# Rows for four more tokens in place of eight in an expert layer, with four buffers for spilled activations

## The chip, the cores and the metric

The kernel runs on one core of a Trainium2 chip. The metric is the device time of one launch in microseconds (us). Before the change the median of three runs is 3247.73 us (3247.13 to 3249.23).

## What is computed

The reference is a decoder trunk of two layers on 512 tokens of width 1024, in float32. Each layer has a block of three attention branches with gates, and then an expert block; the change touches the expert block alone:

```python
def peer_ffn(xn, w_q, k1, k2, u, v):
    # 8 heads, top 16 of 256 candidates each: 128 of 16384 experts for each token
    ...
        ids = jnp.take_along_axis(cand_id, top_pos, axis=-1)
        g = jax.nn.softmax(top_s, axis=-1)
        act = jnp.einsum('thk,td->thk', u[ids], xc, preferred_element_type=jnp.float32)
        w = (g * jax.nn.gelu(act, approximate=False)).astype(v.dtype)
        return jnp.einsum('thk,thkd->td', w, v[ids], preferred_element_type=jnp.float32).astype(xn.dtype)
```

## The kernel before

Each of the 512 tokens uses 128 experts, so for most tokens the kernel computes all 16384 experts densely and multiplies with a gate table that is zero where a token doesn't use an expert. TensorE does this for the first TM = 344 tokens: 344 is the number of columns of each product. The other 168 go "by rows": one indirect DMA by GpSimd gathers 128 rows of `u` or `v` (128x1024 float32, 0.52 MB), and VectorE makes a dot product or an addition of them. The last 128 tokens take one such operation for each of their 128 experts. E = 32 further tokens take 32 (four partitions for each token), and F = 8 more take 8 (16 partitions for each): KF = P // F = 16 copies of the 8 tokens' activations fill the 128 partitions of `x_f`. `row_of` lists these row operations: 2 x (32 + 128 + 8) = 336 in a layer, half with `u`, half with `v`.

A weight chunk holds 256 experts (1 MB). There are 64 up chunks (`u`, then Gelu) and 64 down chunks (`v`), one in each step q of 0 to 127. Every product is three matmuls of float32r parts (hi*hi, hi*lo, lo*hi; `product`, lines 1506 to 1508), 16 products in a chunk, so a chunk is 48 matmuls. Each chunk is loaded by SyncE's queue (`load_raw`) into one of two `raw` buffers when VectorE is done with the chunk two before; ScalarE rounds it to `hi` (`split_hi`, L626), VectorE subtracts (`split_lo`, L983, 2.3 us), then TensorE can use it.

The steps of a layer, by q: 0 to 13 up chunks while the experts are being found; 14 to 42 up chunks with the making of the gate table beside them (three groups of four tokens in a step; a group is two one-hot tables and four 128x128 matmuls, L1815; 86 groups in 29 steps, so the first step has two); 43 to 51 up chunks; then rounds of six down and six up chunks, down at 52 to 57, 64 to 69 and 76 to 81; from 82 on down chunks alone. The Gelu outputs of the first SPILLED = 46 up chunks are spilled to `act_d` in DRAM (`store_act`, 352 KB each); those of the last KEPT = 18 stay in `act_k`, `act_s`, `act_in`. A down chunk needs its activations multiplied by the gates (`weigh_step`), split (`weights_hi` on ScalarE, `weigh_lo` on VectorE) and then TensorE takes them.

SyncE's queue issues in a fixed order. In the down steps from q = 80 on that is: `load_raw` of the chunk, `load_act` of the same chunk's activations into `act_in[s]` (two buffers; it waits until the chunk two before is weighed), and one of four parts of the gates for four chunks (`load_gates`). Before that, `GATES_AT` says at which q parts of gates are loaded; (0, 0) and (0, 2) at 50 and 51 stand for two parts each, so the first block of gates is issued at q = 50 and 51. Four parts have 1.4 MB, in pieces of 1 KB.

VectorE and GpSimd run through the row operations in one fixed order. `rows_by(q)` says how many VectorE has done by the end of step q: 96 of them in steps 14 to 42, and the other 240 in steps 43 to 125 by weights of 16 for an up step and 13 for a down step. GpSimd gathers up to NR = 7 rows ahead: gather n waits until VectorE is done with row n - 7. Before gather n == F_IN = 40 GpSimd issues, in its own instruction order, two small DMAs and the KF loads that make `x_f` (line 606). VectorE waits for a row inside its own stream (`row_op`), in front of the next one-hot tables and the next `split_lo`.

## Time and profile before

| what | before |
|---|---|
| median of three runs | 3247.73 us |
| the profiled execution, as timed | 3249.34 us |
| its span, first to last instruction | 3247.5 us |
| mean granted TensorE clock | 0.998 of 2.4 GHz |
| moved by DMA | 893 MB, mean 275 GB/s |

The profiled execution is 1.6 us longer than the median, and 1.8 us of it lie outside the span. The profile lists for each engine the time in which it was busy, for each idle time the event that ended it, and for each stretch how much was moved by DMA. A matmul's listed duration overlaps the next one's, so the cost of a matmul is read from the distance between two starts in the list by time, not from its duration.

### The profile page before, as it was taken

Reading aid. Unit: us, or ns where it says so; the run is one execution under the profiler, and the core shown is the slowest. Engines: PE = TensorE matmul, PEld = TensorE weight load, DVE = VectorE, ACT = ScalarE, POOL = GpSimd, SP = SyncE. Lnnn points to the kernel's source line nnn. Section 1 sums busy time; section 2 is a strip of 40 time slices with the busy share of each in tenths; the row PEclk is TensorE's granted clock in tenths of the full one; section 3 lists DMA queues with packets and bytes.
Section 4 is the critical chain, followed back from the end, with each engine's and each line's share of the span. In section 5 each row is a group of like instructions: output and inputs, shape, how many; then the busy total and the mean of one; then the engine's idle time right before and its main releaser. Section 6 shows DMA issues by size and latency. Waiting matters only on the chain.

```text
span 3247.5 us, 54682 instructions
## 1 busy us (share of the span) xinstructions
PE 3202.2 (99%) x19694; PEld 3000.9 (92%) x19694; DVE 2597.5 (80%) x4972; ACT 1508.2 (46%) x2298; POOL 1191.4 (37%) x789
## 2 busy tenths in 40 slices
PE   8999999999999999999999999999999999999998
PEld 7878888999999999999988788889999999999998
DVE  6654449999998889999866544499999888999997
ACT  5553233477773333333345532334777633333333
POOL 1000014335435656555300000143454456665552
PEclk9999999999999999999999999999999999999999
DMA  4214422589999999999821143225999999999996
GB/s 148 78 53 143 142 90 91 194 326 386 400 398 399 357 389 390 413 409 416 310 91 66 53 156 130 97 100 189 346 391 393 405 393 370 390 398 417 415 411 258
DMA packets 232172, 893.29 MB, mean 275 GB/s; under 512 B 23856, under 2 KB 69088, under 8 KB 184128
## 3 DMA queue, kind: packets, MB, share of 16 engines
q1 hardware_dynamic: 112912, 455.25, 37.2%
q0 software_dynamic: 99024, 355.98, 27.8%
q10 hardware_dynamic: 20064, 79.91, 6.2%
q8 instruction: 90, 1.47, 0.2%
q14 instruction: 82, 0.67, 0.1%
HBM read 809.57 MB, written 81.48 MB: 274 GB/s over the span
## 4 chain that ended last, share of the span: by engine, by line
PE 63%; issue 14%; DMA 12%; DVE 8%; POOL 2%; ACT 1%; SPq 0%; DVEq 0%; POOLq 0%; ACTq 0%
PE bank L1506 18%; PE bank L1508 18%; PE bank L1507 18%; DMA act_in<-act_d 9%; PE bank L1815 4%; DVE h L1383 4%; DVE w_lo L1411 2%; POOL lo L568 1%; PE bank L1624 1%; PE bank L1661 1%; DMA rows<-in_u_rows,ids 1%; PE bank L1642 1%; DMA raw<-in_stream 1%; DVE lo L983 1%; ACT hi L626 1%
## 5 line engine op out<-in xcount | busy, mean ns | idle before, releaser
L626 ACT ACTIVATE hi<-raw 128x2048 fp32r<-128x2048 f32 (+2 forms) x338 | 620.6, 1836 | 692.9 <-PE bank L1508 396.1
L1506 PE MATMUL bank<-xT_hi,hi 128*128 128x344 f32 (+1 forms) x2688 | 918.7, 342 | 2.1 <-DVE xT_lo L1033 1.7
L1508 PE MATMUL bank<-xT_hi,lo 128*128 128x344 f32 (+1 forms) x2688 | 905.1, 337 | 0.0
L1507 PE MATMUL bank<-xT_lo,hi 128*128 128x344 f32 (+1 forms) x2688 | 900.3, 335 | 0.0
L983 DVE TENSOR_TENSOR lo<-raw,hi 128x2048 fp32r<-128x2048 f32 (+2 forms) x320 | 698.4, 2183 | 183.1 <-ACT hi L626 180.9
L1506 PE MATMUL bank<-w_hi,hi 128*128 128x344 f32 x2048 | 662.3, 323 | 19.2 <-DVE w_lo L1411 18.6
L1507 PE MATMUL bank<-w_lo,hi 128*128 128x344 f32 x2048 | 655.0, 320 | 0.0
L1508 PE MATMUL bank<-w_hi,lo 128*128 128x344 f32 x2048 | 654.0, 319 | 0.0
L615 POOL DMA_INDIRECT rows<-in_v_rows,ids x256 | 426.1, 1665 | 301.6 <-DVE h L1383 248.2
L1506 PEld LDWEIGHTS bank<-xT_hi,hi 128*128 128x128 f32 x2688 | 504.2, 188 | 32.3 <-issue 5.9
L1508 PEld LDWEIGHTS bank<-xT_hi,lo 128*128 128x128 f32 x2688 | 504.4, 188 | 25.3
L1507 PEld LDWEIGHTS bank<-xT_lo,hi 128*128 128x128 f32 x2688 | 505.5, 188 | 22.8
L615 POOL DMA_INDIRECT rows<-in_u_rows,ids x256 | 347.5, 1357 | 349.7 <-DVE act_row L1374 258.5
L1506 PEld LDWEIGHTS bank<-w_hi,hi 128*128 128x128 f32 x2048 | 385.5, 188 | 32.8 <-DVE w_lo L1411 18.7
L1508 PEld LDWEIGHTS bank<-w_hi,lo 128*128 128x128 f32 x2048 | 388.3, 190 | 0.0
L1507 PEld LDWEIGHTS bank<-w_lo,hi 128*128 128x128 f32 x2048 | 385.9, 188 | 0.0
L1383 DVE SCALAR_TENSOR_TENSOR h<-rows,w_row,h 128x1024 f32<-128x1024 f32 x256 | 327.6, 1280 | 7.3
L1374 DVE CUSTOM_DVE_ANT_0 rows<-rows,x_row 128x1024 f32<-128x1024 f32 x256 | 301.3, 1218 | 10.5 <-DMA rows<-in_u_rows,ids 10.1
L1440 DVE TENSOR_SCALAR onehot<-iota_sb,idx1T,gT 128x128 f32<-128x128 f32 x688 | 182.6, 357 | 0.1
L1815 PE MATMUL bank<-onehot 128*128 128x128 f32 x1376 | 172.1, 275 | 0.8 <-DVE onehot L1440 0.8
L1815 PEld LDWEIGHTS bank<-onehot 128*128 128x128 f32 x1376 | 167.7, 191 | 1.1 <-DVE onehot L1440 1.1
L1506 PE MATMUL bank<-hi,xT_hi 128*128 128x448 f32 (+2 forms) x448 | 166.3, 371 | 1.9 <-DVE xT_lo L1033 1.8
(258 smaller groups left out, 4108.8 us busy)
## 6 DMA issues: line engine op xcount, KB each, us to landing
raw<-in_stream SPq DMA_DIRECT2D x352, 1024.0 KB, 7.6
gate_in<-gate_d SPq DMA_DIRECT2D x96, 384.0 KB, 12.4
act_d<-act_s ACTq DMA_DIRECT2D x92, 352.0 KB, 6.3
gate_d<-gate_s ACTq DMA_DIRECT2D x22, 1472.0 KB, 9.6
act_in<-act_d SPq DMA_DIRECT2D x92, 352.0 KB, 10.0
gate_d<-gate_s ACTq DMA_DIRECT2D x22, 576.0 KB, 13.7
gate_in<-gate_d SPq DMA_DIRECT2D x32, 256.0 KB, 9.6
rows<-in_u_rows,ids POOLq DMA_INDIRECT x256, 10.0
```

The source lines that it names most:

```text
L568: pool.tensor_tensor(lo[s][:], raw[s][:], hi[s][:].bitcast(F32), ALU.subtract).then_inc(lo_done, 1)
L615: pool.indirect_dma_start(rows[:, N % NR], None, a["u_rows" if n < U_ROW_OPS else "v_rows"], bass.IndirectOffsetOnAxis(which, 0)).then_inc ...
L626: act.activation(hi[s][:, 0:n], raw[s][:, 0:n], ACT.Copy).then_inc(hi_done, 1)
L983: dve.tensor_tensor(lo[s][:, 0:n], raw[s][:, 0:n], hi[s][:, 0:n].bitcast(F32), ALU.subtract).then_inc(lo_done, 1)
L1374: last = dve.tensor_tensor_reduce(row, row, x_, 1.0, 0.0, ALU.mult, ALU.add, dots[:, k])
L1383: last = dve.scalar_tensor_tensor(out=y_, in0=row, scalar=w_[:, k], in1=y_, op0=ALU.mult, op1=ALU.add)
L1411: dve.tensor_tensor(w_lo[:, s], acts_of(c, s), w_hi[:, s].bitcast(F32), ALU.subtract).then_inc(w_done, 1)
L1440: last = dve.tensor_scalar(o[:, r, 0], iota[:], idx1T[:, t], gT[:, t], ALU.is_equal, ALU.mult)
L1506: pe.matmul(dst, a_[0], b_[0], start=first, stop=False)
L1507: pe.matmul(dst, a_[0], b_[1], start=False, stop=False)
L1508: return pe.matmul(dst, a_[1], b_[0], start=False, stop=last)
L1815: last = pe.matmul(ps[4 + slot][:, tile(r)], o[:, 1], o[:, 0], start=True, stop=True)
```

## The change

`F` goes from 8 to 4. TM becomes 348: every expert product has 348 columns, the gate table has 87 groups, and step 14 has three. KF becomes 32, so `x_f` is made by 32 loads of 4 rows. A layer has 2 x (32 + 128 + 4) = 328 row operations: 98 in steps 14 to 42 and 230 after, by weights of 76 (up), 50 (down, kept) and 49 (down, spilled). F_IN stays 40. The activations' tiles have 352 columns (TU) as before, so that what is spilled, loaded, gated and split keeps its size.

The activations of spilled chunks get four buffers (`act_in` and, after the rounds, `act_k`). SyncE's queue loads the activations of chunk c + 2 behind raw chunk c, each when the chunk four before it is weighed. The first block of gates is loaded at q = 48 and 49 in place of 50 and 51. The Gelu of the row products and their weighing come four steps sooner (66 and 70).

```diff
@@ -99,7 +99,7 @@
 E_TILE, E_ROWS = NDT - 1, slice(P - E, P)
-F = 8
+F = 4
 TM = TU - F
@@ -118,7 +118,7 @@
 U_ROW_OPS = E + P + F
-ROWS_IN_G = 96
+ROWS_IN_G = 98
 OH_PER_LAYER = 2 * G_STEPS - max(G_SHORT, 1) + 1
@@ -145,14 +145,14 @@
 KEPT_ROWS = 2 * KEPT
-SHARED = 2
+SHARED, ACT_BUFS = 2, 4
 BY_ACT, BY_DVE = (0, 2, 4, 5), (1, 3, 6, 7)
-GATES_AT = {50: (0, 0), 51: (0, 2), 52: (1, 0), 53: (1, 1), 54: (1, 2), 55: (1, 3),
+GATES_AT = {48: (0, 0), 49: (0, 2), 52: (1, 0), 53: (1, 1), 54: (1, 2), 55: (1, 3),
             62: (2, 0), 63: (2, 1), 64: (2, 2), 65: (2, 3), 70: (3, 0), 71: (3, 1), 72: (3, 2), 73: (3, 3),
             74: (4, 0), 75: (4, 1), 76: (4, 2), 77: (4, 3)}
-GATES_FROM, V_FROM = 50, 80
-ROW_GELU_AT, WEIGH_ROWS_AT = 70, 74
-UP_SHARE, DOWN_SHARE, ROWS_END = 16, 13, 2 * C_U - 2
+GATES_FROM, V_FROM = 48, 80
+ROW_GELU_AT, WEIGH_ROWS_AT = 66, 70
+UP_SHARE, KEPT_SHARE, DOWN_SHARE, ROWS_END = 76, 50, 49, 2 * C_U - 2
@@ -181,7 +181,7 @@
         return (q - FIND_STEPS) * ROWS_IN_G // (G_STEPS - 1)
-    shares = [UP_SHARE if x in UP_OF else DOWN_SHARE for x in range(FIND_STEPS + G_STEPS, ROWS_END)]
+    shares = [UP_SHARE if x in UP_OF else KEPT_SHARE if DOWN_OF[x] < KEPT else DOWN_SHARE for x in range(FIND_STEPS + G_STEPS, ROWS_END)]
     return ROWS_IN_G + sum(shares[:q + 1 - FIND_STEPS - G_STEPS]) * (ROW_OPS - ROWS_IN_G) // sum(shares)
@@ -450,7 +450,7 @@
-        act_ld = [sem(f"act_ld{s}") for s in range(2)]
+        act_ld = [sem(f"act_ld{b}") for b in range(ACT_BUFS)]
@@ -471,7 +471,17 @@
-            return (act_k, act_s, act_in)[k % SPAN // 2][:, s] if isinstance(k, int) and k < KEPT else act_in[:, s]
+            return (act_k, act_s, act_in)[k % SPAN // 2][:, s]
+        def spilled_acts(b):
+            return (act_in, act_k)[b // 2][:, b % 2]
+        def acts_loaded(l, c):
+            b = c % ACT_BUFS
+            first = KEPT + (b - KEPT) % ACT_BUFS
+            return act_ld[b], 16 * (l * len(range(first, C_V, ACT_BUFS)) + (c - first) // ACT_BUFS + 1)
@@ -484,11 +494,12 @@
                 lp, done = l * PAIRS, l * C_V
-                def load_act(j, s):
+                def load_act(v, x):
+                    j, s, b = v * ACT_BUFS // 2 + x // 2, x % 2, x % ACT_BUFS
                     wait_alone(sp, act_out[s], 16 * (l * ACT_PAIRS + j) + 16, sp_passed)
-                    sp.wait_ge(w_done, done + 2 * j + s + 1)
-                    sp.dma_start(act_in[:, s].rearrange("p i t -> p (i t)"), act_d[2 * j + s - KEPT]).then_inc(act_ld[s], 16)
+                    sp.wait_ge(w_done, done + ACT_BUFS * v + x - ACT_BUFS + 1 + CR)
+                    sp.dma_start(spilled_acts(b).rearrange("p i t -> p (i t)"), act_d[ACT_BUFS * v + x - KEPT]).then_inc(act_ld[b], 16)
@@ -502,8 +513,8 @@
                         load_raw(lp + P_V + v * V_CHUNKS // 2 + c // 2, c % 2)
-                        if not (isinstance(v, int) and v * V_CHUNKS + c < KEPT):
-                            load_act(v * V_CHUNKS // 2 + c // 2, c % 2)
+                        if not last or c + 2 < V_CHUNKS:
+                            load_act(v, c + 2)
                         if not last:
@@ -935,13 +946,14 @@
-                def weights_hi(c, s):
+                def weights_hi(c, s, b):
                     act.wait_ge(prod_done, l * C_V + c + 1)
                         act.wait_ge(w_used, 2 * (lp + P_V) + c + 1)
-                    act.activation(w_hi[:, s], acts_of(c, s), ACT.Copy).then_inc(w_hi_done, 1)
+                    acts = acts_of(c, s) if isinstance(c, int) and c < KEPT else spilled_acts(b)
+                    act.activation(w_hi[:, s], acts, ACT.Copy).then_inc(w_hi_done, 1)
@@ -950,22 +962,22 @@
                     if q + 1 in DOWN_OF:
-                        weights_hi(DOWN_OF[q + 1], (q + 1) % 2)
+                        weights_hi(DOWN_OF[q + 1], (q + 1) % 2, DOWN_OF[q + 1] % ACT_BUFS)
                     if q in UP_OF:
-                def v_steps(j, last_pair=False):
-                    for s in range(2):
-                        if not (last_pair and s == 1):
-                            ahead(lp + P_V + j, s)
-                            weights_hi(2 * j + s + 1, 1 - s)
-                with act.Fori(KEPT // 2, C_V // 2 - 1) as j:
-                    v_steps(j)
-                v_steps(C_V // 2 - 1, True)
+                def v_steps(v, first, end):
+                    for x in range(first, end):
+                        ahead(lp + P_V + v * ACT_BUFS // 2 + x // 2, x % 2)
+                        weights_hi(v * ACT_BUFS + x + 1, (x + 1) % 2, (x + 1) % ACT_BUFS)
+                v_steps(KEPT // ACT_BUFS, KEPT % ACT_BUFS, ACT_BUFS)
+                with act.Fori(KEPT // ACT_BUFS + 1, C_V // ACT_BUFS - 1) as v:
+                    v_steps(v, 0, ACT_BUFS)
+                v_steps(C_V // ACT_BUFS - 1, 0, ACT_BUFS - 1)
                 if l + 1 < DEPTH:
@@ -1398,9 +1410,10 @@
                     else:
-                        dve.wait_ge(act_ld[s], 16 * (l * ACT_PAIRS + (c - KEPT) // 2 + 1))
+                        dve.wait_ge(*acts_loaded(l, c))
                     dve.wait_ge(gate_ld[v % 2], 16 * GATE_PARTS * (v // 2 + 1))
-                    a_ = acts_of(c, s).rearrange("p i (q t) -> p i q t", t=SLICE)
+                    acts = acts_of(c, s) if c < KEPT else spilled_acts(c % ACT_BUFS)
+                    a_ = acts.rearrange("p i (q t) -> p i q t", t=SLICE)
                     i = 2 * (c % V_CHUNKS)
@@ -1408,7 +1421,8 @@
                     dve.wait_ge(w_hi_done, k + 1)
-                    dve.tensor_tensor(w_lo[:, s], acts_of(c, s), w_hi[:, s].bitcast(F32), ALU.subtract).then_inc(w_done, 1)
+                    acts = acts_of(c, s) if c < KEPT else spilled_acts(c % ACT_BUFS)
+                    dve.tensor_tensor(w_lo[:, s], acts, w_hi[:, s].bitcast(F32), ALU.subtract).then_inc(w_done, 1)
```

## Rows read from the trace of the kernel before

**Rows 1.** The page's part 1: busy us, share of the span, instructions

```profile
PE 3202.2 (99%) x19694; PEld 3000.9 (92%) x19694; DVE 2597.5 (80%) x4972; ACT 1508.2 (46%) x2298; POOL 1191.4 (37%) x789
```

**Rows 2.** List by time, TensorE (start, us): starts 27 apart, then 57 apart

```profile
249.72 0.39 PE L1508 MATMUL bank<-oT_hi,lo 128*128 128x512 f32 x1
...
255.84 0.39 PE L1508 MATMUL bank<-xT_hi,lo 128*128 128x512 f32 x1
...
1043.80 0.32 PE L1506 MATMUL bank<-w_hi,hi 128*128 128x344 f32 x1
...
1052.73 0.32 PE L1506 MATMUL bank<-w_hi,hi 128*128 128x344 f32 x1
```

**Rows 3.** Stretches of steps 14-42, 43-51, 84-125: busy us (x), clock, DMA, GB/s

```profile
662.00:960.00 298.00, 297.21 (x2088) 296.93 (x2086) 287.06 (x612) 235.61 (x472) 138.10 (x122) 1.00 0.99 385
960.00:1033.00 73.00, 68.35 (x434) 68.06 (x432) 53.77 (x66) 26.34 (x29) 34.10 (x30) 0.99 1.02 413
1280.00:1600.00 320.00, 315.15 (x1978) 309.25 (x1977) 295.76 (x237) 111.71 (x83) 180.87 (x111) 1.00 1.02 409
```

**Rows 4.** List by time, TensorE: starts of step 76 and behind 127, both layers

```profile
1217.06 0.42 PE L1506 MATMUL bank<-w_hi,hi 128*128 128x344 f32 x1
...
1620.40 1.31 PE L1914 MATMUL bank<-ident_sb,gate_in 128*128 128x128 f32 x10 [0.38 <-PE bank L1508]
...
2831.22 0.42 PE L1506 MATMUL bank<-w_hi,hi 128*128 128x344 f32 x1
...
3232.71 1.53 PE L1914 MATMUL bank<-ident_sb,gate_in 128*128 128x128 f32 x12 [0.38 <-PE bank L1508]
```

**Rows 5.** Waits, steps 76 to 126, layer 0: us, times, longest

```profile
ACT hi L626 <- DMA raw<-in_stream: 120.2, 27, 6.0
DVE act_in L1406 <- DMA act_in<-act_d: 24.1, 18, 3.0
PEld bank L1506 <- DVE w_lo L1411: 10.3, 17, 1.9
```

**Rows 6.** DMA issues, steps 84 to 125: count, KB, median us to landing

```profile
act_in<-act_d SPq DMA_DIRECT2D x41, 352.0 KB, 10.1
```

**Rows 7.** List by time, TensorE: two gate groups of one step

```profile
670.10 1.83 PE L1815 MATMUL bank<-onehot 128*128 128x128 f32 x15
```

**Rows 8.** List by time, GpSimd: x_f loads, row gather 40, both layers

```profile
776.98 8.20 POOL L606 DMA_DIRECT2D x_f<-f_x_d  x16
785.48 1.00 POOL L615 DMA_INDIRECT rows<-in_u_rows,ids  x1 [0.30 <-issue]
...
2394.66 8.00 POOL L606 DMA_DIRECT2D x_f<-f_x_d  x16
2402.96 1.14 POOL L615 DMA_INDIRECT rows<-in_u_rows,ids  x1 [0.30 <-issue]
```

**Rows 9.** List by time, VectorE: row operation 40, both layers

```profile
796.74 1.23 DVE L1374 CUSTOM_DVE_ANT_0 rows<-rows,x_row 128x1024 f32<-128x1024 f32 x1 [3.48 <-DMA rows<-in_u_rows,ids]
...
2412.27 1.22 DVE L1374 CUSTOM_DVE_ANT_0 rows<-rows,x_row 128x1024 f32<-128x1024 f32 x1 [1.37 <-DMA rows<-in_u_rows,ids]
```

**Rows 10.** List by time, TensorE: before step 27's first gate matmul, layer 0

```profile
798.55 0.32 PE L1508 MATMUL bank<-xT_hi,lo 128*128 128x344 f32 x1
799.66 0.38 PE L1815 MATMUL bank<-onehot 128*128 128x128 f32 x1 [0.79 <-DVE onehot L1440]
```

**Rows 11.** List by time, TensorE: first matmul of step 52, both layers

```profile
1033.20 0.62 PE L1506 MATMUL bank<-w_hi,hi 128*128 128x344 f32 x1 [4.85 <-DVE w_lo L1411]
...
2649.56 0.40 PE L1506 MATMUL bank<-w_hi,hi 128*128 128x344 f32 x1 [4.58 <-DVE w_lo L1411]
```

**Rows 12.** Stretches behind these two waits, columns as in Rows 3

```profile
1033.20:1041.00 7.80, 7.80 (x34) 7.80 (x35) 7.80 (x11) 2.71 (x2) 5.39 (x3) 0.65 0.99 357
2649.40:2653.40 4.00, 3.84 (x15) 3.87 (x16) 4.00 (x8) 1.91 (x1) 1.73 (x2) 0.57 1.00 383
```

**Rows 13.** Chain that ended last (start, us, what): load of chunk 52

```profile
1010.29 17.70 DMA raw<-in_stream
```

## The prediction

> **What bounds the kernel now.** I read the page's engine totals first: TensorE is busy for 99% of the span, VectorE for 80% [rows 1]. A matmul's listed time overlaps the next one's, so that share hides short stalls and tells nothing of the cost of a column. For that I read the list by time on TensorE: 27 matmuls of 512 columns start in 6.12 us, 0.2267 us apart, and 57 of 344 columns in 8.93 us, 0.1567 us apart [rows 2]. The slope is (0.2267 - 0.1567) / 168 = 0.417 ns a column, one column in a cycle of 2.4 GHz. A free chunk of 48 matmuls takes 7.52 us, and wherever chunks come faster than that nothing else can help.
>
> So I looked for stretches with more than 7.52 us a chunk. The three stretches by window show PE full in steps 14 to 42, 4.7 us short in steps 43 to 51, and 4.9 us short in steps 84 to 125, where DMA runs at 409 GB/s with all engines busy [rows 3]. The 52 chunks from step 76 to the end take 403.3 and 401.5 us in the two layers (1217.06 to 1620.40, 2831.22 to 3232.71) [rows 4], where 52 x 7.52 is 391.0: 12.3 and 10.5 us are lost, 22.8 in all. The waits of that stretch name who is late: ScalarE waits 120 us for raw chunks, VectorE 24 us for spilled activations, and TensorE 10 us for `w_lo` at the end of that row [rows 5]. An activation load lands 10.1 us after its issue [rows 6].
>
> **Wider products.** 64 up and 64 down chunks of 48 matmuls in two layers are 12288 matmuls; 4 columns more are 1.67 ns each: +20.5 us. TensorE is the bound in nearly all of them, so nothing hides this. The 87th group falls in step 14, eight matmuls at about 0.11 us: +0.9 us in each layer, +1.8 [rows 7]. VectorE's extra one-hot table there lies before TensorE comes to it or costs some tenths, taken as nothing.
>
> The Trainium skill, page "TensorE: Matmul & The Clock Gate", section "Back-to-back issue gap", gives sustained spacings of 81 ns at 128 and 131 ns at 512 columns in a stream of loads and matmuls. By those, 4 columns would be 0.5 ns and the whole term 6.4 us. This case's trace doesn't agree: its 227 ns at 512 columns and its slope of one column a cycle stand against it [rows 2].
>
> **The long down stretch.** A step of spilled down chunks moves a raw chunk of 1.05 MB, activations of 0.36, gates of 0.36, and its rows. By the shares of before (21 up steps of 16, 62 down steps of 13, 240 rows) a down step has 2.73 rows, 1.43 MB: 3.20 MB in 7.52 us would be 426 GB/s, more than the 409 that the stretch got [rows 3]. After (21 x 76, 18 x 50, 44 x 49, 230 rows) it has 2.42 rows, 1.27 MB: 3.04 MB in a chunk of 7.60 us, 400 GB/s, just under. VectorE, busy for 92% of it [rows 3], loses 0.3 row operations a step. And the four buffers start each activation load two chunks, some 15 us, before the old point, against 10.1 us to landing [rows 6]; the load stands in the same place of SyncE's queue and waits for the same weighing, so no raw load behind it is held longer. With DMA at 98% of what it reached, some lateness stays: I take 3 us in each layer. -22.8 + 6 = -16.8. Bounds: -22.8 (all gone) and 0 (raw was the late one and stays so).
>
> **The x_f loads.** This is the part I think decides. GpSimd issues 16 loads of `x_f` in 8.20 and 8.00 us, and only then row gather 40 [rows 8]. VectorE comes to row 40 before it has landed, and waits 3.48 and 1.37 us [rows 9]. In layer 0 that wait reaches TensorE: its first gate matmul of step 27 starts at 799.66 after the matmul of 798.55, 1.11 us where 0.16 is normal, with VectorE's one-hot as the releaser [rows 10]. So VectorE's lead is 3.48 - 1.0 = 2.5 us. After the change there are 32 such issues. They are half as large, but 0.51 us is the time of the issuing instruction and not of the transfer, so I add 8.2 and 8.0 us; if an issue cost as its rows do, it would be nothing, which is the lower end. The Trainium skill, page "DMA: Bandwidth & Descriptors", section "Anatomy of one DMA — SWDGE (gpsimd) path", calls the generation of descriptors a small part of a DMA's fixed time, of which many can be made before their cost shows; the trace has loads of one size alone here, so it can't tell. By the new counts row 32, which releases gather 39, is the second row of its step, not the third, and row 40 is wanted third, not fourth: both move alike. VectorE waits 11.7 and 9.4 us, less about 1 for a gather that lands sooner behind a lull: 10.7 and 8.4. Behind that wait in VectorE's stream stand the one-hot tables of the next step and `split_lo`, so TensorE stalls by the wait less the lead: 8.2 and 5.9, +14.1 less the 1.0 there now: +13.1 us. Bounds: 0 (the rows were further ahead than I think) and +17.
>
> A stall of that size lowers the clock. TensorE stood 4.85 and 4.58 us before step 52 [rows 11], and the stretches behind have a granted clock of 0.65 and 0.57 [rows 12]: 34 matmuls in 7.8 us where 50 fit, 15 in the 3.84 us where 24 fit. That costs 16 and 9 x 0.157: 2.5 and 1.4 us. I count one such fall: +2.0, with 0 and 4 as bounds. That is the lower of the two levels, 1.2 GHz, for part of each stretch.
>
> **Steps 43 to 57.** The chain shows why TensorE stood there: raw chunk 52, issued at 1010.29, took 17.7 us to land [rows 13]. Ahead of it in SyncE's queue were the four parts of the first gate block, 1.4 MB in pieces of 1 KB, and DMA ran at 413 GB/s all through [rows 3]. Moving this block two steps forward takes it away from chunk 52 and puts it before chunks 49 to 51, in the same full stretch, which now has 33 rows in place of 30: 1.57 MB, 3.8 us at 413 GB/s. Most of the stall moves to about step 50; a part is hidden by the slack that the chunks had there. I take each stall about 1 us shorter and one of the two clock falls gone: -2 - 2 = -4. Bounds: -14 (both stalls and falls gone: 4.85 + 4.58 + 3.9) and +8 (the added bytes are paid in full).
>
> The up steps 70 to 75 have four parts of gates and 22 rows, not 20: 1.05 MB more, 2.6 us at 409. Seven gathers in flight cover most: +1.5 for both layers (0 to 5). Gelu and weighing of the row products four steps sooner still stand behind the rows that they need: nothing. Unrolling ScalarE's loop to four: nothing.
>
> **The sum**, against the profiled execution of 3249.3 us (1.6 over the median): 20.5 + 1.8 - 16.8 + 13.1 + 2.0 - 4.0 + 1.5 = +18.1, so 3267.4 there and 3247.7 + 18.1 = 3265.8 us as a median.
>
> **The rivals.**
> A. *The x_f loads stay covered.* GpSimd starts them sooner, or the issues are shorter. For it: in layer 1 the wait of now is only 1.37 us. Against: an added 8 us exceeds lead and all. Without 13.1 and 2.0 it is +3.0: 3250.7.
> B. *The stall before step 52 vanishes and does not come back at 50.* For: the 4.7 us that TensorE is short in the stretch [rows 3] are this one gap [rows 11], so all chunks up to 51 were in time while 1.4 MB of gates were being asked for. Against: the stretch is full. A further -10: 3255.8.
> C. *The other side: A and B at once.* The moved block clears step 52, the rows are ahead, and the down stretch runs free. Then -22.8 - 14.2 + 22.3 + 1.5 = -13.2 at best, -7.2 with 3 us of lateness in each layer: 3240.5. It wins if VectorE's wait at row 40 stays below its lead of 2.5 us and raw chunks 49 to 52 all land within two steps of their issue.
> D. *The denser up steps overload DMA.* 3.8 us in steps 43 to 51 and 2.6 us in 70 to 75 are paid in full in each layer, and the falls of the clock stay: about +12 on the sum: 3278.
> E. *The four buffers don't do what they say.* Raw chunks are the ones that are late (120 us against 24 [rows 5]), and lateness falls by the bytes alone, half: +5: 3271.
> F. *Cheaper columns*, by the spacing of a stream in which loads and matmuls overlap: 0.13 ns a column in place of 0.417, 14.1 us less: 3251.7. The measured slope speaks against it [rows 2].
>
> **How the numbers follow.** Forecast 0.40, A 0.17, B 0.13, C 0.09, D 0.12, E 0.07, F 0.02. A measurement can tell about 0.2%, 6.5 us, from no change: the bounds are 3241.2 and 3254.2. Faster: C, 0.09, and 0.01 of A: 0.10. Same: the rest of A and F: 0.18. Slower: 0.72. The range leaves out most of C and the far end of D: 3243 to 3283.
>
> **What would show it.** Starts of matmuls 0.1583 us apart; TensorE's gap in step 26 or 27, with the one-hot table as releaser and VectorE waiting 8 to 11 us for row 40 behind 16.4 us of `x_f` issues; a raw chunk between 49 and 51 late in place of 52; VectorE's waits for activations gone in the down stretch, its 52 chunks in 396 to 399 us. The forecast is wrong if VectorE waits under 3 us at row 40, if no chunk before 58 is late, or if the down stretch stays over 401 us.

## The result, and the profile after

The median went from 3248.5 to 3274.3 us (four runs each): a ratio of 1.0085, with a 95% interval of 1.0072 to 1.0098. The change makes the kernel slower by 26 us, where 18 were forecast. All the stretches below are of the profiled executions, 3247.5 and 3271.1 us in span, 23.6 apart. Two of the experiments had one execution each at a much lower granted clock (4549 us at 0.65 and 5122 us at 0.57 of full), and the times given leave these two out.

The totals of the page (columns as in [rows 1]) and its chain by engine say little. TensorE is at 98%, with 16 us more, for two layers of an added gate group and four more columns in each product:

```profile
PE 3217.9 (98%) x19710; PEld 3027.9 (93%) x19710; DVE 2582.5 (79%) x4958; ACT 1499.1 (46%) x2300; POOL 1185.5 (36%) x805
...
PE 80%; issue 7%; DVE 6%; DMA 3%; POOL 2%; ACT 1%; ACTq 0%; POOLq 0%; DVEq 0%
```

The starts of matmuls tell more. I cut the lists by time of both kernels where the kind of chunk changes. For the long down stretch the rows of after that answer to [rows 4] are these (start us, us):

```profile
1234.69 0.32 PE L1520 MATMUL bank<-w_hi,hi 128*128 128x348 f32 x1
...
1630.56 1.64 PE L1928 MATMUL bank<-ident_sb,gate_in 128*128 128x128 f32 x13 [0.38 <-PE bank L1522]
...
2860.32 0.32 PE L1520 MATMUL bank<-w_hi,hi 128*128 128x348 f32 x1
...
3256.20 0.98 PE L1928 MATMUL bank<-ident_sb,gate_in 128*128 128x128 f32 x7 [0.38 <-PE bank L1522]
```

The 52 chunks take 395.87 and 395.88 us, where they took 403.3 and 401.5 with narrower products. The stretch gained 13.1 us, and what lies ahead of it lost more:

| steps | before, layers 0 and 1 | after | change, both | what changed |
|---|---|---|---|---|
| 0 to 13 | 107.2, 107.2 | 107.5, 107.5 | +0.6 | columns |
| 14 to 42 | 297.5, 296.5 | 306.8, 305.2 | +18.1 | a stall before step 27 |
| 43 to 51 | 73.3, 73.0 | 76.0, 76.1 | +5.9 | two stalls in place of one |
| 52 to 57 | 47.7, 46.8 | 45.6, 45.6 | -3.3 | clock fall gone |
| 58 to 63 | 45.4, 44.2 | 50.0, 50.1 | +10.5 | a new stall before step 64 |
| 64 to 69 | 45.1, 45.2 | 48.0, 47.2 | +4.9 | its clock fall |
| 70 to 75 | 45.6, 45.6 | 45.6, 45.6 | 0.0 | |
| 76 to 127 | 403.3, 401.5 | 395.9, 395.9 | -13.1 | DMA keeps up |

The sum is +23.6, the difference of the spans.

**The stall before step 27.** GpSimd's list by time after, the rows that answer to [rows 8] in layer 0:

```profile
778.37 16.19 POOL L617 DMA_DIRECT2D x_f<-f_x_d  x32
794.87 1.01 POOL L626 DMA_INDIRECT rows<-in_u_rows,ids  x1 [0.30 <-issue]
```

VectorE's list by time, row operation 40 in both layers, as in [rows 9]:

```profile
801.04 1.23 DVE L1386 CUSTOM_DVE_ANT_0 rows<-rows,x_row 128x1024 f32<-128x1024 f32 x1 [7.12 <-DMA rows<-in_u_rows,ids]
...
2428.34 1.23 DVE L1386 CUSTOM_DVE_ANT_0 rows<-rows,x_row 128x1024 f32<-128x1024 f32 x1 [6.51 <-DMA rows<-in_u_rows,ids]
```

TensorE's list, before the first gate matmul of step 27, as in [rows 10]:

```profile
800.65 0.32 PE L1522 MATMUL bank<-xT_hi,lo 128*128 128x348 f32 x1
806.11 2.07 PE L1829 MATMUL bank<-onehot 128*128 128x128 f32 x8 [5.14 <-DVE onehot L1454]
```

Thirty-two issues take 16.19 us, 0.51 each. Gather 40 comes behind them, VectorE waits 7.12 us for it, and TensorE stands from 800.65 to 806.11. The gap is 5.5 us, and 5.1 in layer 1 (2428.30 to 2433.43).

**The stall before step 64** was not foreseen. First the chain of waits of the changed kernel there (start us, us, what):

```profile
1123.48 1.07 issue
1124.54 12.23 DMA rows<-in_v_rows,ids_e
...
1136.80 1.28 DVE rows L1395
```

Then VectorE's list by time:

```profile
1136.80 1.28 DVE L1395 SCALAR_TENSOR_TENSOR rows<-rows,w_e 128x1024 f32<-128x1024 f32 x1 [3.06 <-DMA rows<-in_v_rows,ids_e]
1138.00 2.28 DVE L995 TENSOR_TENSOR lo<-raw,hi 128x2048 fp32r<-128x2048 f32 x1
```

And TensorE's, with the first matmul of step 64:

```profile
1136.61 0.32 PE L1522 MATMUL bank<-xT_hi,lo 128*128 128x348 f32 x1
1141.14 0.66 PE L1520 MATMUL bank<-w_hi,hi 128*128 128x348 f32 x1 [4.21 <-DVE w_lo L1425]
```

A gather lands 12.2 us after its issue, VectorE waits 3.06 us for it with the raw chunk's `lo` and then `w_lo` behind it in its stream, and TensorE waits 4.2 us for `w_lo`. Why this gather was asked for so late stands in GpSimd's list:

```profile
1100.22 0.95 POOL L626 DMA_INDIRECT rows<-in_u_rows,ids  x1 [6.94 <-issue]
1101.47 2.91 POOL L626 DMA_INDIRECT rows<-in_u_rows,ids  x1 [0.30 <-issue]
1104.69 1.98 POOL L626 DMA_INDIRECT rows<-in_u_rows,ids  x1 [0.30 <-issue]
...
1124.54 0.95 POOL L626 DMA_INDIRECT rows<-in_v_rows,ids_e  x1 [0.30 <-issue]
```

From 1100.22 on GpSimd waits for nobody: it issues 12 gathers in 24.32 us, one in 2.03 us, each instruction 0.95 to 2.9 us long. Steps 58 to 63 want 23 rows in 45.6 us, one in 1.98 us. The kernel before issues the same 12 gathers in 24.87 us, with one wait of 1.1 us for VectorE among them:

```profile
1097.85 0.94 POOL L615 DMA_INDIRECT rows<-in_u_rows,ids  x1 [1.46 <-issue]
...
1122.72 1.91 POOL L615 DMA_INDIRECT rows<-in_u_rows,mx  x1 [0.30 <-issue]
```

but it wants 20 rows, one in 2.27 us, and keeps up. So the new weights of 76, 50 and 49 ask GpSimd for more than it issued there in either kernel. Over steps 58 to 63 DMA isn't full. By window (columns as in [rows 3]) it moves 351 GB/s, but far from evenly:

```profile
1091.20:1141.10 49.90, 45.73 (x289) 45.44 (x288) 38.48 (x49) 19.13 (x20) 33.27 (x22) 0.98 0.93 351
1100.20:1108.00 7.80, 7.80 (x51) 7.80 (x51) 6.78 (x10) 2.94 (x4) 6.86 (x4) 1.00 0.67 231
1130.00:1136.80 6.80, 6.80 (x44) 6.64 (x42) 3.42 (x7) 2.78 (x3) 4.61 (x4) 1.00 1.02 415
```

My working looked at bytes and at VectorE, and never at GpSimd's pace. The pace isn't all of the stall, though. The missing 0.05 us a gather make 0.6 us in 12; GpSimd is some 2.3 us late already at 1100.22 (as it is at the same gather in the kernel before, 1097.85; no row says why); and the gather that VectorE waits for lands 11.3 us after the end of its issuing instruction, where the 12 before it were in use after 5.4 to 8.7 us. While it is under way DMA is full (the last of these windows), after a lull with GpSimd late (the second). In layer 1 the gather in question is issued 1.1 us after VectorE frees its buffer, the usual lag, and lands late all the same, with DMA full there too (413 GB/s from 2749.80 to 2756). That the dense rows cause the stall is tested below; how much of it is late issue and how much late landing on a full DMA is not.

**Why a gather's issue is sometimes long** stands in the same lists. VectorE runs a `split_lo` there when the gather of 2.91 us is issued:

```profile
1101.27 2.29 DVE L995 TENSOR_TENSOR lo<-raw,hi 128x2048 fp32r<-128x2048 f32 x1 [1.02 <-ACT hi L637]
```

It ends at 1103.56, and the gather's instruction at 1104.38, 0.82 us later. That is the rule of the whole trace: 457 gathers of the changed kernel begin while VectorE is in an instruction with two tensor inputs that has 0.25 us or more to run, and 448 of them end 0.75 to 0.9 us after that instruction does (487 of 498 in the kernel before). Those issued with VectorE idle take 0.95 us (28 of them, at most 1.01), and so do the 80 beside one-hot tables of L1454, which have one tensor input (at most 1.06). So GpSimd's pace depends on VectorE's load, and a denser step slows the gathers that it needs more of.

**The other stretches** by window, in the columns of [rows 3]: steps 14 to 42, 43 to 51, 64 to 69 and the middle of the down stretch.

```profile
662.70:969.50 306.80, 301.56 (x2091) 300.99 (x2089) 290.67 (x618) 235.74 (x472) 145.83 (x140) 0.99 0.97 376
969.50:1045.60 76.10, 72.18 (x436) 71.62 (x435) 58.61 (x74) 26.00 (x29) 48.60 (x33) 0.96 1.02 406
1141.10:1189.10 48.00, 47.96 (x289) 47.96 (x290) 42.82 (x35) 13.40 (x12) 24.28 (x17) 0.95 0.94 348
1286.00:1608.00 322.00, 322.00 (x2035) 322.00 (x2034) 289.64 (x232) 109.58 (x85) 160.95 (x101) 1.00 1.01 396
```

The last row answers to the last of [rows 3]: TensorE is busy in all of 322 us, and DMA moves 396 GB/s, not 409. (Both windows end in steps that load less; the experiment with the old weights compares equal steps.) In the waits of that stretch ScalarE now waits for TensorE (222.7 us, in 45 waits) and no longer for raw chunks, and VectorE for no activation at all:

```profile
ACT hi L637 <- PE bank L1522: 222.7, 45, 5.1
POOL rows L626 <- DVE h L1395: 143.4, 47, 5.2
```

### The profile page after: what moved, and what is told of

Its sections match the earlier page's. It is cut to its first block, busy times and chain, and to the rows that moved or that the text cites. A ratio compares the mean times of both kernels' runs of the same rounds, so it can differ in the third digit from the quotient of the medians.

```text
span 3271.1 us, 54598 instructions
## 1 busy us (share of the span) xinstructions
PE 3217.9 (98%) x19710; PEld 3027.9 (93%) x19710; DVE 2582.5 (79%) x4958; ACT 1499.1 (46%) x2300; POOL 1185.5 (36%) x805
## 4 chain that ended last, share of the span: by engine, by line
PE 80%; issue 7%; DVE 6%; DMA 3%; POOL 2%; ACT 1%; ACTq 0%; POOLq 0%; DVEq 0%
PE bank L1520 24%; PE bank L1521 23%; PE bank L1522 23%; PE bank L1829 4%; DVE lo L995 2%; DMA rows<-in_u_rows,ids 2%; POOL lo L579 1%; DVE rows L1386 1%; PE bank L1638 1%; PE bank L1675 1%; PE bank L1656 1%; DMA raw<-in_stream 1%; DMA rows<-in_v_rows,ids_e 1%; ACT hi L637 1%; DVE onehot L1454 1%
## 5 line engine op out<-in xcount | busy, mean ns | idle before, releaser
L1520 PE MATMUL bank<-xT_hi,hi 128*128 128x348 f32 (+1 forms) x2688 | 925.3, 344 | 11.6 <-DVE lo L995 9.6
L1521 PE MATMUL bank<-xT_lo,hi 128*128 128x348 f32 (+1 forms) x2688 | 908.9, 338 | 0.0
L1522 PE MATMUL bank<-xT_hi,lo 128*128 128x348 f32 (+1 forms) x2688 | 908.7, 338 | 0.0
L1520 PE MATMUL bank<-w_hi,hi 128*128 128x348 f32 x2048 | 654.6, 320 | 8.5 <-DVE w_lo L1425 8.5
L1521 PE MATMUL bank<-w_lo,hi 128*128 128x348 f32 x2048 | 660.3, 322 | 0.0
L1522 PE MATMUL bank<-w_hi,lo 128*128 128x348 f32 x2048 | 658.3, 321 | 0.0
L626 POOL DMA_INDIRECT rows<-in_v_rows,ids x256 | 417.2, 1630 | 343.6 <-DVE h L1395 286.8
L626 POOL DMA_INDIRECT rows<-in_u_rows,ids x256 | 357.3, 1396 | 326.9 <-DVE act_row L1386 221.9
L1454 DVE TENSOR_SCALAR onehot<-iota_sb,idx1T,gT 128x128 f32<-128x128 f32 x696 | 183.8, 358 | 0.0
```

The source lines that it names most:

```text
L626: pool.indirect_dma_start(rows[:, N % NR], None, a["u_rows" if n < U_ROW_OPS else "v_rows"], bass.IndirectOffsetOnAxis(which, 0)).then_inc ...
L1454: last = dve.tensor_scalar(o[:, r, 0], iota[:], idx1T[:, t], gT[:, t], ALU.is_equal, ALU.mult)
L1520: pe.matmul(dst, a_[0], b_[0], start=first, stop=False)
L1521: pe.matmul(dst, a_[0], b_[1], start=False, stop=False)
L1522: return pe.matmul(dst, a_[1], b_[0], start=False, stop=last)
```

## The experiments

I start with the two stalls that decide the sign, take the gains and the columns after them, and end with versions that mend what was found. Ratios are to the kernel before on the same chip. Its median there was between 3246.1 and 3248.5 us, so differences between two experiments, or from the changed kernel's 3274.3, are uncertain by some 2 to 5 us.

### One load for x_f

The changed kernel, with one DMA that reads `f_x_d` 32 times in place of 32 DMAs:

```diff
-                        for kf in range(KF):
-                            pool.dma_start(x_f[kf * F:(kf + 1) * F], f_x_d).then_inc(f_x_in, 16)
+                        pool.dma_start(x_f[:], bc(f_x_d, 0, KF)).then_inc(f_x_in, 16)
...
-            dve.wait_ge(f_x_in, 16 * KF * (l + 1))
+            dve.wait_ge(f_x_in, 16 * (l + 1))
```

> The kernel after, with one load in place of the 32 that fill x_f: its source is the four rows in DRAM, repeated 32 times by the access pattern. Theory (the 32 issues on GpSimd hold up row gather 40, and that reaches TensorE): VectorE's wait of 7.1 us at row 40 and TensorE's gaps of 5.46 and 5.13 us before step 27 go, and with them the two falls of the clock behind them (2.6 and 1.5 us): about 14 us less than the kernel after, near 3260. Rival (the 0.5 MB of x_f or the gathers' own latency holds row 40, not the issues): the wait at row 40 stays over 3 us and less than 5 us are won.

3261.1 us, 1.0036 (1.0021 to 1.0051): 13.2 us less than the changed kernel. GpSimd's list by time at the place:

```profile
778.32 0.59 POOL L616 DMA_DIRECT2D x_f<-f_x_d  x1
779.21 1.01 POOL L625 DMA_INDIRECT rows<-in_u_rows,ids  x1 [0.30 <-issue]
```

and TensorE's:

```profile
800.81 0.32 PE L1521 MATMUL bank<-xT_hi,lo 128*128 128x348 f32 x1
800.97 1.05 PE L1828 MATMUL bank<-onehot 128*128 128x128 f32 x8
```

The one issue takes 0.59 us and gather 40 starts 15.7 us sooner. The gate matmul of step 27 follows its predecessor by 0.16 us, in both layers. The stall before step 64 stays (gaps of 6.4 and 4.8 us), so the two have separate causes. In the profiled executions steps 14 to 42 are 14.4 us shorter, which is the two gaps (5.3 + 5.0 over the normal 0.16) and their clock falls; 2.6 of that are lost again in steps 58 to 69. By the ratios, 1.0085 and 1.0036, the saving is 16 us.

### The issues counted, on the kernel before

The kernel before with each of its 16 loads split into two of half the rows, 32 issues in all:

```diff
-                        for kf in range(KF):
-                            pool.dma_start(x_f[kf * F:(kf + 1) * F], f_x_d).then_inc(f_x_in, 16)
+                        for kf in range(2 * KF):
+                            pool.dma_start(x_f[kf * F // 2:(kf + 1) * F // 2], f_x_d[kf % 2 * F // 2:(kf % 2 + 1) * F // 2]).then_inc(f_x_in, 16)
...
-            dve.wait_ge(f_x_in, 16 * KF * (l + 1))
+            dve.wait_ge(f_x_in, 32 * KF * (l + 1))
```

> The kernel before, with each of its 16 loads of x_f split in two of four rows: 32 issues, the same bytes, nothing else changed. Theory (a load's cost on GpSimd is its issue, 0.5 us whatever its size): GpSimd spends 16.2 us on them, VectorE waits 7 to 11 us at row 40, TensorE stalls 5 to 8 us before step 27 in each layer with a fall of the clock behind: 11 to 15 us slower than the kernel before, near 3261. Rival (only together with the new counts of rows does it reach TensorE): under 4 us.

3262.3 us, 1.0051 (1.0034 to 1.0068): 16 us more than before (11 to 22 by the interval), from 16 added issues of the same bytes in all. So it is the number of issues that costs, at half the size and without four tokens less. The prediction had 13.1 for the stalls and 2.0 for their clock falls. No trace shows where the 16 us lie: the one kept is of the execution of 4549 us. It shows GpSimd's issues, though, and the 64 loads of four rows in its two layers take 0.52 us each (median), as the 32 of eight rows in the kernel before do.

### The old weights of the rows

The changed kernel with the shares of before, and Gelu and weighing of the row products back at 70 and 74:

```diff
-UP_SHARE, KEPT_SHARE, DOWN_SHARE, ROWS_END = 76, 50, 49, 2 * C_U - 2
-ROW_GELU_AT, WEIGH_ROWS_AT = 66, 70
+UP_SHARE, KEPT_SHARE, DOWN_SHARE, ROWS_END = 16, 13, 13, 2 * C_U - 2
+ROW_GELU_AT, WEIGH_ROWS_AT = 70, 74
```

> The kernel after, with the row shares of before (16 for up steps, 13 for down steps; Gelu and weighing of the row products at steps 70 and 74 again). Theory (the new stalls of 4.4 and 4.5 us before step 64 come from up steps with 3.8 rows each): both go with their clock falls (2.3 and 1.6 us), and the stalls of steps 43 to 51 shrink by some us; the down stretch, now with 2.6 rows a step (3.12 MB in 7.6 us, 411 GB/s), loses 2 to 5 us in each layer again: 5 to 12 us less than the kernel after, 3262 to 3269. Rival (these stalls come from the four-buffer change or the gate loads at steps 62 and 63): they stay, and the time is that of the kernel after or more.

3259.7 us, 1.0042 (1.0028 to 1.0056): 14.6 us less than the changed kernel. Steps 58 to 63 have 20 rows again, and chunks come without a gap into step 64 (TensorE's list; the step's first matmul is the last row):

```profile
1134.61 0.32 PE L1522 MATMUL bank<-xT_hi,lo 128*128 128x348 f32 x1
1134.77 0.32 PE L1520 MATMUL bank<-w_hi,hi 128*128 128x348 f32 x1
```

Each round of six chunks takes 45.60 us in both layers. The stall before step 27 stays (5.4 us in both layers). Of the saving 12.9 us lie in steps 58 to 69 (profiled executions). The weights and the steps of Gelu and weighing went back together, but the stall stood before step 64, ahead of both places of the Gelu (66 and 70), so it came of the weights.

The down stretch stays free, 395.74 us in both layers, although it has more rows than the changed kernel: 116 in steps 82 to 125, not 107. The expectation of 2 to 5 us of loss in each layer failed. So the weights of 76, 50 and 49 cost 13 to 15 us and bought nothing. Steps 84 to 119 of layer 0 by window, first of the kernel before, then of this one:

```profile
1278.50:1558.40 279.90, 275.66 (x1730) 270.36 (x1729) 258.20 (x207) 97.55 (x72) 161.35 (x99) 1.00 1.03 412
1286.80:1560.40 273.60, 273.60 (x1730) 273.60 (x1730) 253.28 (x203) 93.62 (x72) 163.06 (x96) 1.00 1.03 414
```

DMA moves 414 GB/s here and TensorE loses nothing, so 409 GB/s was no ceiling. By the prediction's sum these steps ask for 3.15 MB in 7.60 us, 415 GB/s, and are free; the kernel before asked for 426 and was bound.

### Loads of gates near the new stall, moved away

The other suspect for the stall before step 64 were the parts of gates at 62 and 63:

```diff
-            62: (2, 0), 63: (2, 1), 64: (2, 2), ...
+            56: (2, 0), 57: (2, 1), 64: (2, 2), ...
```

> The kernel after, with the two parts of gates of steps 62 and 63 loaded at steps 56 and 57, where DMA is not full; the row shares stay as they are. Theory (3.8 rows a step are more than GpSimd issues in time: a gather takes 1.9 us of it there): the stalls before step 64 stay at 3.5 us or more, within 4 us of the kernel after. Rival (the gate loads in their small pieces, beside dense rows, make the row and raw chunk late): the stalls before step 64 fall under 1.5 us in both layers, and 8 to 13 us are won with the clock falls.

3275.0 us, 1.0089 (1.0072 to 1.0106), and the gaps before step 64 are 4.9 and 4.3 us, where the changed kernel has 4.5 and 4.7. These two parts of gates are not the cause.

### The first block of gates back at 50 and 51

```diff
-GATES_AT = {48: (0, 0), 49: (0, 2), ...
+GATES_AT = {50: (0, 0), 51: (0, 2), ...
-GATES_FROM, V_FROM = 48, 80
+GATES_FROM, V_FROM = 50, 80
```

> The kernel after, with the first block of gates at steps 50 and 51 as before. Theory (moving the block only moves the stall, since DMA is full from step 43 to 52 and the rows are denser): the gaps at steps 47 to 51 go, one gap of 5 to 8 us stands before step 52, and the total stays within 4 us of the kernel after. Rival (the move itself was worth what the stall before step 52 cost): 6 to 12 us slower than the kernel after.

3280.8 us, 1.0108 (1.0091 to 1.0126): 6.5 us more than the changed kernel. TensorE's first matmul of step 52, in the form of [rows 11]:

```profile
1046.30 0.63 PE L1520 MATMUL bank<-w_hi,hi 128*128 128x348 f32 x1 [6.52 <-DVE w_lo L1425]
```

Without the move the denser up steps would have made the stall before step 52 6.5 us long, with 5.5 in layer 1, and smaller ones before it. So the move is worth 6.5 us (6.6 by the profiled executions, 7.5 by the ratios); with it the debt is paid in two parts, before steps 47 and 50.

### Wider products alone

The kernel before with 348 columns in each expert product; the four added columns are computed and not used:

```diff
-product(ps[i][:, 0:TM], ..., at(xT, kk, slice(0, TM)), ...
+product(ps[i][:, 0:TM + 4], ..., at(xT, kk, slice(0, TM + 4)), ...
-product(ps[d][:, 0:TM], ..., at((w_hi, w_lo), s, i, slice(0, TM)), ...
+product(ps[d][:, 0:TM + 4], ..., at((w_hi, w_lo), s, i, slice(0, TM + 4)), ...
```

> The kernel before, with products of 348 columns in place of 344 in all expert chunks and nothing else changed (the four more columns are of a token that is computed by rows as well, and are not used). By the prediction's slope of 0.417 ns a column: +20.5 us, less what the down stretch hides, where 48 columns' worth of stalls stood: 13 to 20 us. By the spacings read off the kernel after (157.8 to 158.3 ns in up chunks, 156.7 to 158.3 ns in down chunks): +3 us in the up chunks and +2 us in the down chunks outside the long down stretch, and 0 to 8 in it: 5 to 13 us.

3253.9 us, 1.0020 (1.0010 to 1.0029): +7.1 us, a third of the 20.5 in the sum (3 to 9 by the interval). Two reasons. In the down stretch the columns are hidden. The list by time gives its first matmul and the first behind it:

```profile
1217.69 0.43 PE L1506 MATMUL bank<-w_hi,hi 128*128 128x348 f32 x1
...
1621.50 0.76 PE L1914 MATMUL bank<-ident_sb,gate_in 128*128 128x128 f32 x5 [0.38 <-PE bank L1508]
```

That is 403.8 us against 403.3 of before, where 2496 matmuls by 1.67 ns would add 4.2: a stretch bound by DMA takes wider products for nothing. And in up chunks four columns cost less than four cycles. The 672 matmuls of steps 0 to 13 start at 554.29 in the kernels before and after. The first transpose behind them starts here in the kernel before (a row not shown yet):

```profile
661.52 0.30 PE L1803 MATMUL bank<-ident_sb,idx_t 128*128 128x128 f32 x1 [0.51 <-issue]
```

and here in the changed kernel:

```profile
661.81 0.30 PE L1817 MATMUL bank<-ident_sb,idx_t 128*128 128x128 f32 x1 [0.44 <-issue]
```

0.29 us in 672 matmuls is 0.43 ns each, not 1.67. Up chunks of 344 columns had a spacing of about 157.8 ns, 1.1 more than the 156.7 of down chunks [rows 2]; with 348 both kinds have 158.3 (rounds of 288 matmuls in 45.60 us). In the changed kernel 57 down matmuls take 9.02 us, 158.2 ns each:

```profile
1045.57 0.32 PE L1520 MATMUL bank<-w_hi,hi 128*128 128x348 f32 x1
...
1054.59 0.32 PE L1520 MATMUL bank<-w_hi,hi 128*128 128x348 f32 x1
```

### Four buffers alone

The kernel before with four activation buffers and everything else old (8 tokens, gates at 50, old weights; the diff of the change without the edits of `F`, `ROWS_IN_G`, `GATES_AT`, the shares and `ROW_GELU_AT`):

```diff
-SHARED = 2
+SHARED, ACT_BUFS = 2, 4
```

> The kernel before (eight tokens, 344 columns, its row shares and gate steps) with the four activation buffers alone. Theory A (the late activation loads and what queues behind them cost the down stretch its 12.3 and 10.5 us, not the bytes): the 52 chunks take 391 to 393 us and the time is about 20 us under the kernel before. Theory B (the bytes bound that stretch: 3.20 MB in a chunk of 7.52 us would be 426 GB/s where DMA gave 409): the 52 chunks still need 3.20 MB / 409 GB/s = 7.8 us each while rows are gathered, raw chunks stay late, and less than 8 us are won.

3247.8 us, 1.0002 (0.9992 to 1.0012): nothing. The waits of the down stretch (us, times, longest) show why:

```profile
ACT hi L637 <- DMA raw<-in_stream: 217.8, 43, 7.2
```

VectorE's waits for activations, 24 us before [rows 5], are gone; ScalarE's waits for raw chunks went from 120 to 218 us. The 52 chunks take 401.7 and 401.1 us. The transfers change places and the bytes stay, so TensorE stands as long as before.

### Eight tokens with the repairs

The kernel before with four buffers, the gates at 48 and 49 (`GATES_FROM` 48) and one load for `x_f`:

```diff
-SHARED = 2
+SHARED, ACT_BUFS = 2, 4
-GATES_AT = {50: (0, 0), 51: (0, 2), ...
+GATES_AT = {48: (0, 0), 49: (0, 2), ...
-                        for kf in range(KF):
-                            pool.dma_start(x_f[kf * F:(kf + 1) * F], f_x_d).then_inc(f_x_in, 16)
+                        pool.dma_start(x_f[:], bc(f_x_d, 0, KF)).then_inc(f_x_in, 16)
```

> The kernel before (eight tokens, 344 columns, its row shares) with four activation buffers, the first block of gates at steps 48 and 49, and x_f filled by one load. If each part acts by itself: 20 us for the buffers, 4 to 8 for the moved gates, 2 for the load: 3216 to 3222, faster than the kernel before by 0.8%. Rival (with eight tokens the denser rows of the down stretch, 2.7 a step, keep it bound by DMA): over 3232.

3245.6 us, 0.9999 (0.9990 to 1.0009). Its down stretch takes 402.5 and 400.5 us. With chunks of 7.52 us and 2.73 rows a step it stays bound by DMA, with four buffers as with two.

### Four tokens with both repairs

The changed kernel with the one load and the old weights, that is both of these edits:

```diff
-                        for kf in range(KF):
-                            pool.dma_start(x_f[kf * F:(kf + 1) * F], f_x_d).then_inc(f_x_in, 16)
+                        pool.dma_start(x_f[:], bc(f_x_d, 0, KF)).then_inc(f_x_in, 16)
-UP_SHARE, KEPT_SHARE, DOWN_SHARE, ROWS_END = 76, 50, 49, 2 * C_U - 2
-ROW_GELU_AT, WEIGH_ROWS_AT = 66, 70
+UP_SHARE, KEPT_SHARE, DOWN_SHARE, ROWS_END = 16, 13, 13, 2 * C_U - 2
+ROW_GELU_AT, WEIGH_ROWS_AT = 70, 74
```

> The changed kernel with both repairs: x_f by one load, and the old shares of rows (16, 13, 13) with the Gelu and weighing of the row products at 70 and 74. Theory: the two causes are independent, the one before step 27 and the other before step 64, so the savings of 13.2 and 14.6 us add up: 3274.3 - 27.8 = 3246.5 us, level with the kernel before (within 0.2%). Rival: they share a loss (clock falls counted in both, or a stall that is free to move behind), so that the sum gives only some 20 us: 3254. In the trace the gaps before steps 27 and 64 are both gone under the theory, the 52 chunks from step 76 take 395.8 us in each layer, and what is left is one or two gaps of 1 to 5 us in steps 43 to 51.

3242.3 us, 0.9988 (0.9979 to 0.9997): 32.0 us less than the changed kernel. The savings add up, and some 2 us (by the ratios) to 4 us (by the medians) come on top. Both gaps are gone in both layers, and the down stretch takes 395.74 us in each. What is left are gaps of 1.2 and 3.3 us in steps 43 to 51 (1.0 and 3.0 in layer 1), smaller than with either repair alone (4.6 and 5.3 us for the larger one with the one load, 3.5 and 4.8 with the old weights).

### The same with two buffers

The kernel before with one load for `x_f` and

```diff
-F = 8
+F = 4
-ROWS_IN_G = 96
+ROWS_IN_G = 98
-GATES_AT = {50: (0, 0), 51: (0, 2), ...
+GATES_AT = {48: (0, 0), 49: (0, 2), ...
-GATES_FROM, V_FROM = 50, 80
+GATES_FROM, V_FROM = 48, 80
```

It differs from the last kernel in the buffers alone.

> The kernel before with only this of the change: four tokens in place of eight (348 columns, 87 groups), and gates at 48 and 49; x_f by one load; its two activation buffers and its shares 16 and 13 stay. It differs from the kernel with both repairs in the buffers alone. Theory: the long down stretch is bound by bytes, and wider chunks with fewer rows are what freed it, not the buffers: its 52 chunks take under 397 us in each layer with two buffers too, and the time is within 3 us of the kernel with both repairs, 3246.5. Rival: with two buffers the activations are late (VectorE waited 24 us for them in the kernel before), and TensorE loses 2 to 4 us in each layer: 399 us or more for the 52 chunks, 3252.

3243.7 us, 0.9992 (0.9983 to 1.0001). The down stretch takes 395.8 us in layer 0 and 397.8 in layer 1, with one gap of 1.6 us. The four buffers are worth 0 to 2 us, within what these runs can tell; wider chunks with fewer rows freed the stretch.

### Fewer rows in the up steps

The same as the kernel with both repairs, but with the weights

```diff
-UP_SHARE, KEPT_SHARE, DOWN_SHARE, ROWS_END = 16, 13, 13, 2 * C_U - 2
+UP_SHARE, KEPT_SHARE, DOWN_SHARE, ROWS_END = 15, 14, 13, 2 * C_U - 2
```

> The changed kernel with x_f by one load and shares 15, 14, 13 (up, kept down, spilled down) in place of 76, 50, 49, with Gelu and weighing of the row products at 70 and 74. Steps 43 to 51 then have 27 rows in place of 33 (29 by the old shares), steps 58 to 63 have 18 in place of 23, the kept down steps 17 in place of 15. Theory: the stall that is left in steps 43 to 51 is paid by bytes, so 2 rows less than with the old shares, 1.05 MB, give back up to 2.5 us in each layer, and the kept down steps have room for theirs: 3242 us, faster than before by 0.1 to 0.2%. Rival: a gather comes too late in the denser kept steps 52 to 57 or 64 to 69, VectorE waits there, and a new gap of 2 to 4 us opens before one of the steps 53 to 58 or 65 to 70: 3250.

3236.4 us, 0.9969 (0.9958 to 0.9980): 9.6 us faster than the kernel before, and 37.9 faster than the changed one. Steps 43 to 51 with 27 rows, and the down stretch, by window (columns as in [rows 3]):

```profile
961.60:1032.10 70.50, 68.76 (x434) 68.35 (x433) 52.05 (x64) 25.99 (x28) 32.21 (x27) 1.00 1.00 399
1280.00:1600.00 320.00, 320.00 (x2023) 320.00 (x2022) 296.67 (x237) 109.15 (x84) 173.97 (x105) 1.00 0.99 398
```

One gap is left in each layer, 2.06 and 2.30 us, and no fall of the clock comes behind it: the granted clock is 1.00, where the kernel with both repairs lost some 1.7 us in each layer. It beats both kernels of the case, and none here was faster by more than the noise.

### Still fewer

```diff
-UP_SHARE, KEPT_SHARE, DOWN_SHARE, ROWS_END = 15, 14, 13, 2 * C_U - 2
+UP_SHARE, KEPT_SHARE, DOWN_SHARE, ROWS_END = 14, 15, 13, 2 * C_U - 2
```

This gives 25 rows in steps 43 to 51, 89 and not 87 in steps 52 to 81.

> The kernel with the shares 15, 14, 13 once more, with 14, 15, 13: steps 43 to 51 have 25 rows in place of 27, steps 52 to 81 have 89 in place of 87, the stretch of spilled down chunks 116 as before. Steps 43 to 51 have gaps of 2.06 and 2.30 us left with 27 rows (3.3 to 4.6 with 29). Theory: they are paid by bytes, so 2 rows less, 1.05 MB or 2.5 us at 413 GB/s, take away all that is left: no gap over 0.3 us in steps 43 to 51 of either layer, 68.5 us for their nine chunks in place of 70.6 and 70.8, and 3236.4 - 4.4 = 3232 us. Rival: what is left comes of the four parts of the first block of gates, issued at steps 48 and 49 in 1 KB pieces ahead of a raw chunk, and not of the rows: gaps of 1.5 us or more stay in each layer and the time is within 2 us of 3236.4, or the denser steps 52 to 81 open a new gap and it is above that.

3237.0 us, 0.9966 (0.9954 to 0.9978), so no gain over the last. The theory holds by halves. The gaps in steps 43 to 51 shrink from 2.06 and 2.30 to 0.94 and 1.81, by 1.6 us in all and not to nothing, and the raw chunks of the down stretch are late again. ScalarE's waits in layer 0, from step 76 on:

```profile
ACT hi L636 <- DMA raw<-in_stream: 167.6, 32, 7.2
```

The stretch takes 397.6 and 396.8 us, 2.9 more in the two layers. Its rows per step from 82 on are the same 116; steps 76 to 81 have 19 in place of 17. The debt was moved, not paid.

## Why the prediction was right, and where it wasn't

Direction and range hold; the forecast was +18.1, and +25.8 came. That the total came so near is in part luck: the columns were 7 us too high, a stall of 12.8 us was missing, and steps 43 to 57 were 5 us too low. Step by step, in us for both layers:

| term | forecast | measured | from |
|---|---|---|---|
| columns | +20.5 | about +13.5 | spacings: 0.55 ns in 6144 up, 1.6 to 1.7 ns in 6144 down matmuls |
| 87th group | +1.8 | about +1.8 | eight matmuls (not four, as the description of the kernel says) 0.11 us apart, two layers |
| long down stretch | -16.8 | -21.1 | -13.1 net, with 8.0 of columns paid in it |
| x_f stalls | +13.1 | +9.3 | gaps 5.3 + 5.0, less 1.0 of before |
| their clock falls | +2.0 | +4.2 | two falls, not one |
| steps 43 to 57 | -4.0 | +1.2 | +2.6 in the table above, less 1.4 of columns |
| steps 70 to 75 | +1.5 | 0 | 45.6 us in both kernels |
| before step 64, with its falls | not seen | +12.8 | 4.4 + 4.5 of gaps, 3.9 behind them |

These add up to +21.7 where the spans differ by 23.6. Of the 1.9 left, 1.3 are a fast stretch of before (its steps 58 to 63 took 44.2 us in layer 1, 153.3 ns a matmul) and the rest lies in tenths in steps 14 to 42. What caused the fast stretch is open.

**The x_f loads** were called the part that decides. The place, the releaser and the 0.51 us for each issue came as said [rows 8], and both experiments on it agree: one load takes 13.2 us away, 16 more issues cost the kernel before 16. The size was off. VectorE was to wait 10.7 us in layer 0 and waited 7.12 and then 0.91 for the next row. GpSimd's loads end 9.4 us later (794.56 against 785.18), but gather 40 then took 6.2 us from issue to VectorE's start, where it had taken 11.3 (785.48 to 796.74). I had put what a gather gains behind such a lull at 1 us; it is 5. The lead of 2.5 us was right: TensorE lost 5.3 of the 8.0 us, a lead of 2.7. In layer 1 it was 7.5 us of waits for 5.0 of gap, a lead of 2.5.

**The columns.** The slope of one column a cycle was taken between 344 and 512 columns of different streams. Between 344 and 348 it holds for down chunks (1.6 ns for four) and not for up chunks, whose 344 had been slower than its size. That is the direction of rival F, a cheaper column, for a third of the term, and not by its mechanism: nothing here comes near the 131 ns at 512 columns of the Trainium skill, page "TensorE: Matmul & The Clock Gate", section "Back-to-back issue gap" (227 ns here [rows 2]). The other thing that failed is "nothing hides this": in the long down stretch DMA did.

**The long down stretch** came out as worked out: full before, not full after, 3 us of lateness allowed and 0.7 found in each layer. Two steps of the working were off. The buffers were given a part in it, and four buffers alone gave 0 (1.0002), at four tokens 0 to 2 us; the bytes term alone carries the gain. And the 409 GB/s taken for the limit were the mean of a window with lighter steps at its end: with the old weights the stretch ran free at 414 GB/s. Eight tokens with 348 columns (2.73 rows in 7.60 us, 421 GB/s by the same sum) stayed bound, so of what the change does here the small step from 2.73 to 2.64 rows, together with wider products, was enough. Rival E was right that raw chunks were the late ones, and wrong in its price, for it didn't see that bytes alone would free the stretch.

**Steps 43 to 57.** The stall moved to step 50, as the forecast said and B denied, but only half of it in layer 0 and two thirds in layer 1, the rest to step 47 (before 47 and 50: 2.3 and 2.2 us in layer 0, 2.3 and 4.0 in layer 1). The larger of layer 1 has its clock fall, and so has each of layer 0, so that nothing was saved on falls. The move as such was worth 6.5 us; the three more rows took as much (with the gates at 50 these steps take 248.9 us in both layers, in the kernel before 240.7, and 1.4 of that are columns). The step that failed is "a part is hidden by the slack that the chunks had there".

**Before step 64** the method failed. I costed the denser up steps in bytes (rival D: 3.8 and 2.6 us at 413 and 409 GB/s) and looked at 43 to 51 and 70 to 75, while 58 to 63, with 23 rows for 20, stood in no sum at all. And DMA's bytes alone don't explain it (351 GB/s on the mean there, 231 in one part): as far as the rows tell GpSimd's issue fell behind, one in 2.03 us against one wanted in 1.98, and the gathers then came late into a DMA that was full for the last 12 us. The row for it was in the trace of before: gathers with instruction times from 0.95 to 3 us. D's total of 3278 was near what came, in other steps and by a mechanism that is at most in part D's.

Rivals A and C are out: VectorE waited 7 us at row 40. The kernel with both repairs comes to 3242.3, near C's 3240.5, but that is luck in part: its steps 43 to 51 still have gaps of 4 us in each layer, which C had at none, and its columns cost 7 us less than C's sum had. Two edits of the change, the 32 loads and the weights, took 32 us away.

## What to carry to other kernels

Count DMAs by issue and not by bytes on an engine that also feeds the critical path: 16 small loads more on GpSimd cost the kernel before 16 us, and one load with a repeated source did the work of all 32 in the changed one and gave 13 back. When work is redistributed over steps, check each step's pace against every engine in its chain (here rows a step against GpSimd's issue), not only against bandwidth. In the stretch that was bound by bytes here, wider products were nearly free (+0.5 us in 403.3), and more buffers gave nothing.
